# Six weight slots in place of four, with the low half of a weight unit written over its landed values

## The chip, the cores and the metric

One core of one Trainium2 chip runs the whole program. The metric is the device time of one execution, in microseconds (us). Matrix products run on TensorE (PE), copies and exponentials on ScalarE (ACT), elementwise work and reductions on VectorE (DVE) and GpSimd (POOL), and SyncE (SP) issues nearly all transfers from device memory. Every engine works through its own list of instructions in order and waits on semaphores where its program says so.

## The reference

Two layers, each with a combined input projection, three token mixers side by side, an output projection with a layer norm, and a squared-ReLU MLP with another. There are 512 tokens of width 1024, the input projection is 2578 wide, and the MLP 4096. Cut to what matters:

```python
for l in range(DEPTH):                                  # 2
    proj = jnp.einsum('btd,dn->btn', x, w_in[l])        # 1024 x 2578
    (qa, ka, va, u, qc, kcm, vcm, ksl, vsl, kwi, vwi, gc) = jnp.split(proj, offsets, axis=-1)
    qa = apply_rope(...); ka = apply_rope(...)
    o_a = diff_attention(qa[:, :, 0], qa[:, :, 1], ka[:, :, 0], ka[:, :, 1], va, lam, lam_init, subln_g[l])
    o_b = pool_mixer(u, w_pool[l], pool_scale[l])
    qc, kcm, ksl, kwi = (apply_rope(...) for each)
    o_c = nsa_attention(qc, kcm, vcm, ksl, vsl, kwi, vwi, gates, cmp_pe_k[l], cmp_pe_v[l], w_cmp_k[l], w_cmp_v[l])
    mix = jnp.einsum('btm,md->btd', jnp.concatenate([o_a, o_b, o_c], axis=-1), w_out[l])   # 1024 x 1024
    x = layer_norm(ALPHA * x + mix, ln1_g[l], ln1_b[l])
    hid = jnp.square(jax.nn.relu(jnp.einsum('btd,df->btf', x, w_up[l])))                   # 1024 x 4096
    x = layer_norm(ALPHA * x + jnp.einsum('btf,fd->btd', hid, w_down[l]), ln2_g[l], ln2_b[l])
```

`diff_attention` subtracts two causal softmaxes, weighted by `lam`, before it multiplies with the values. With 512 tokens, `N_SEL` covers every block and the window every key, so the selected and the window branch are plain causal attention.

## The kernel before

**Precision.** Every large product is made of three: a value is split into a high part (`w_hi`, `xt_hi`, rounded to the matmul's type) and a low part (value minus high part), and PE adds high x low, high x high and low x high.

**Weight units.** The weights of a layer are cut into 96 units (`UNITS`) of 256 rows by 430 columns (input projection, units 0 to 23) or by 512 (output projection 24 to 31, MLP 32 to 95). Four units make a chunk of output columns. A unit goes through three places: SP loads it into `raw` (L398 to L420), ACT writes `w_hi` from it (`split_to`, L880 to L888), and POOL writes `w_lo` as `raw` minus `w_hi` (`split`, L483 to L490). Each of the three has `RING` = 4 slots of 4 KB per partition, and unit g (counted through both layers) uses slot g modulo `RING`. Units 26, 27, 30 and 31 are loaded in three, two, three and two transfers, the others in one.

**What frees a slot.** Before the change, the load of unit g waits until POOL has written the low part of unit g-4 (`s_lo_ready`); ACT and POOL wait until PE has used unit g-4 (`s_unit_used`, one count for each unit that PE is through with). The program writes "PE is through with n units" as `unit_used` n; so here below too, counted within the layer.

**Order on ACT.** In the input projection (L936 to L945) step n first splits all units below n+`RING` and then, where n is a multiple of four or one more (from 4 on), copies two of the four PSUM banks of the chunk that PE has ended (`copy_in`). At n = 4, ahead of the splits of that step, it copies the turned parameters to `lnp` and `pe_t` (L939, L940); PE waits for that before its second chunk (L807). The last chunk's four banks follow (L946 to L951), then two copies to `ka` (L956), one exponential of `lams` (L959), the splits up to `U_OUT + RING` (L960), and then the attention tasks, of which `exps(t)` is the first part of each.

**Order on DVE.** DVE rotates the positions (`rotate`) of the A heads after the second chunk is copied, and those of the C heads after the fifth chunk is copied (L1180). Behind that come the copies of the turned queries and keys (L1189, L1191), two small operations on `lams` (L1194, L1195) and then `negative_max(0)` and `(1)` (L1201), for which the first `exps` wait. `weights(t)` (L1246 for the first member of a pair, L1244 for the second) scales the probabilities.

**Order on POOL.** It splits the units up to `U_OUT + RING` and then makes the rows for the compressed keys and values (`rows_to_compress`, L508), rotations, box sums and masks during attention. In the MLP loop ACT splits one unit and copies one block of the hidden layer (L1067) in turns.

Of the kernel before, what the change touches and what calls it, by code (L numbers as in the profile page):

```python
# [16 lines left out]
F32R = mybir.dt.float32r  # L17
# [40 lines left out]
IN_W, IN_CHUNKS = 430, 6  # L58
U_IN, U_OUT, U_MLP = 0, 24, 32
UNITS = U_MLP + 4 * N_MLP  # L60
RING = 4
TURN_BANK = (4, 0)

PARTS = ((0, 1), (2,), (3,))
# [84 lines left out]
def pieces(u):  # L149

    return {U_OUT + 2: 3, U_OUT + 3: 2, U_OUT + 6: 3, U_OUT + 7: 2}.get(u, 1)
# [20 lines left out]
def build(nc, x, w_in, lam_q1, lam_k1, lam_q2, lam_k2, subln_g, w_pool, pool_scale, cmp_pe_k, cmp_pe_v,  # L172
          w_cmp_k, w_cmp_v, w_out, ln1_g, ln1_b, w_up, w_down, ln2_g, ln2_b, consts, out):
    ctx = ExitStack()
    with ctx:
        top = [16512]

        def at(name, offset, shape, dt=F32):

            return nc.alloc_sbuf_tensor_at(name, [P] + list(shape), dt, offset=offset)  # L180

        def room(nbytes):
            top[0] += nbytes
            return top[0] - nbytes

        def sb(name, shape, dt=F32):
            size = int(np.prod(shape)) * (2 if dt == BF16 else 4)
            return at(name, room((size + 31) // 32 * 32), shape, dt)
# [5 lines left out]
        ident16 = sb("ident16", [P], BF16)  # L194
        mask16 = sb("mask16", [P], BF16)
        xres = sb("xres", [TT, D])
        raw = sb("raw", [RING, 1024])
        w_hi = sb("w_hi", [RING, 1024], F32R)
        w_lo = sb("w_lo", [RING, 1024], F32R)

        ra = room(32768)
        xt_hi, xt_lo = at("xt_hi", ra, [KT, SEQ], F32R), at("xt_lo", ra + 16384, [KT, SEQ], F32R)
# [64 lines left out]
        def sem(name):  # L267
            return ctx.enter_context(nc.semaphore(name))

        def raw_landed(layer, u):  # L270

            before = layer * sum(pieces(v) for v in range(u % RING, UNITS, RING))
            return 16 * (before + sum(pieces(v) for v in range(u % RING, u + 1, RING)))

# [3 lines left out]

        s_raw = [sem(f"raw{r}") for r in range(RING)]
        s_ident_in = sem("ident_in")  # L280
# [10 lines left out]
        s_lo_ready = sem("lo_ready")  # L291
        s_unit_used = sem("unit_used")
# [62 lines left out]
        def unit_of(ring, u):  # L355

            return ring[:, u % RING].rearrange("p (k c) -> p k c", k=2)[:, :, 0:unit_width(u)]

        def unit_source(layer, u):
            kind, c = CHUNKS[u // 4]  # L360
            r = 256 * (u % 4)
            if kind == "in":
                src = w_in[layer, r:r + 256, IN_W * c:IN_W * c + unit_width(u)]
            elif kind == "out":
                src = w_out[layer, r:r + 256, 512 * c:512 * c + 512]
            elif kind == "up":
                src = w_up[layer, r:r + 256, 512 * c:512 * c + 512]
            else:
                r += 1024 * (c // 2)
                src = w_down[layer, r:r + 256, 512 * (c % 2):512 * (c % 2) + 512]  # L370
            return src.rearrange("(k p) c -> p k c", p=P)
# [27 lines left out]
        def _(sp):  # L399
            sp.dma_start(ident, consts[:, K_ID:K_ID + P]).then_inc(s_ident_in, 16)  # L400
            def unit(layer, u):
                g = layer * UNITS + u
                if g >= RING:

                    sp.wait_ge(s_lo_ready, g - RING + 1)
                to = unit_of(raw, u)
                cols = slice(512 * CHUNKS[u // 4][1], 512 * CHUNKS[u // 4][1] + 512)
                if pieces(u) == 1:
                    sp.dma_start(to, unit_source(layer, u)).then_inc(s_raw[u % RING], 16)
                elif pieces(u) == 3:  # L410

                    sp.dma_start(to[:, 0], w_out[layer, 512:640, cols]).then_inc(s_raw[u % RING], 16)
                    for hh in range(2):
                        r = 640 + 192 * hh
                        sp.dma_start(to[64 * hh:64 * hh + 64, 1], w_out[layer, r:r + 64, cols]).then_inc(s_raw[u % RING], 16)
                else:
                    for hh in range(2):
                        r = 704 + 192 * hh
                        sp.dma_start(to[64 * hh:64 * hh + 64], w_out[layer, r:r + 128, cols].rearrange("(k p) c -> p k c", p=64)) \
                            .then_inc(s_raw[u % RING], 16)  # L420

            for layer in range(DEPTH):
                for u in range(RING):
                    unit(layer, u)
                    if layer == 0 and u == 0:
                        for tt in range(TT):
                            sp.dma_start(xres[:, tt], x[0, tt * P:(tt + 1) * P, :]).then_inc(s_x_in[tt], 16)
# [25 lines left out]
                for u in range(RING, UNITS):  # L453
                    if u == 3 * RING:
                        if layer:

                            sp.wait_ge(s_out_normed, nth("out_normed", layer - 1, TT))
                        else:

                            sp.wait_ge(s_masks, 1)  # L460
                        sp.dma_start(cmp_kw[:, :, 1, :], w_cmp_v[layer].rearrange("(j h) d e -> (h d) j e", h=2)) \
                            .then_inc(s_value_weights, 16)
                    unit(layer, u)
# [915 lines left out]
```

## Time and profile before

| | |
|---|---|
| time, median of 3 runs | 1374.91 us (1374.71 to 1378.96) |
| the profiled execution's own time | 1374.61 us |
| its span from the first to the last instruction | 1372.8 us |
| PE busy | 1290.0 us (94%) |
| DVE busy | 728.4 us (53%) |
| POOL busy | 568.6 us (41%) |
| ACT busy | 486.3 us (35%) |
| DMA moved | 110.03 MB, 80 GB/s on average |

The time and the span are 1.8 us apart. A share of busy time is an average over stages that have different limits: in the projections and the MLP PE works without a gap, in the attention (about 128 to 285 us and 804 to 965 us) and around the layer norms it waits for others. Times in the views count from the start of the span. "Granted clock" is the share of TensorE's full 2.4 GHz that the chip allowed in a stretch: 1.00 or, at the lower level of 1.2 GHz, 0.50.

### The profile page before, as it was taken

What the parts mean: (1) busy time and instruction counts of PE and PEld (TensorE: products, weight loads), DVE (VectorE), ACT (ScalarE), POOL (GpSimd) and SP (SyncE); (2) the same over time, 40 slices, a digit from 0 to 9 for tenths busy, and PEclk for the clock granted to TensorE, in tenths of its full rate; (3) what the DMA queues carried; (4) which work ended last, traced back from release to release, by engine and by line L of the source; (5) the groups of instructions that cost most, each with busy time, mean ns of one, the idle gap of its engine ahead of it and who ended that gap; (6) DMA issues with size and microseconds to landing.
All of it is one profiled execution on the core that took longest, in us unless ns stands there. A gap on an engine that the chain in (4) does not pass through costs nothing.

```text
span 1372.8 us, 17332 instructions
## 1 busy us (share of the span) xinstructions
PE 1290.0 (94%) x6834; PEld 1060.2 (77%) x6834; DVE 728.4 (53%) x1107; ACT 486.3 (35%) x1016; POOL 568.6 (41%) x320
## 2 busy tenths in 40 slices
PE   7999878998999999999989978899989999999996
PEld 6998545687888888888889965556888888888885
DVE  4234796717865063360495077866288641623506
ACT  4234557713322222221233345586233222222211
POOL 4443840033644444444355449100436444444444
PEclk9999689999999999999999987799999999999998
DMA  7432100021422322322144320000314232233211
GB/s 253 117 95 76 33 1 1 1 93 62 137 94 93 105 94 93 103 97 90 39 131 111 98 78 0 1 1 1 111 43 154 92 106 95 93 102 98 93 62 61
DMA packets 66656, 110.03 MB, mean 80 GB/s; under 512 B 14928, under 2 KB 27536, under 8 KB 66448
## 3 DMA queue, kind: packets, MB, share of 16 engines
q1 hardware_dynamic: 65424, 104.74, 24.5%
q10 hardware_dynamic: 1152, 4.19, 0.9%
q8 instruction: 54, 0.88, 0.3%
q14 instruction: 26, 0.21, 0.1%
HBM read 106.82 MB, written 2.10 MB: 79 GB/s over the span
## 4 chain that ended last, share of the span: by engine, by line
PE 86%; DVE 9%; ACT 2%; POOL 1%; issue 1%; DMA 1%; SPq 0%; POOLq 0%; ACTq 0%; DVEq 0%
PE ps L650 16%; PE ps L651 16%; PE ps L652 16%; PE ps L646 8%; PE ps L648 8%; PE ps L647 8%; PE ps L709 3%; PE ps L701 3%; DVE probs_a L1244 2%; PE ps L745 2%; DVE negmax L1201 1%; PE ps L605 1%; PE ps L730 1%; DVE xres L1111 1%; DVE probs_a L1246 1%; PE ps L761 1%
## 5 line engine op out<-in xcount | busy, mean ns | idle before, releaser
L489 POOL TENSOR_TENSOR w_lo<-raw,w_hi 128x1024 fp32r<-128x1024 f32 (+2 forms) x192 | 461.8, 2410 | 709.8 <-ACT w_hi L887 709.7
L887 ACT ACTIVATE w_hi<-raw 128x1024 fp32r<-128x1024 f32 (+2 forms) x192 | 196.4, 1026 | 619.8 <-PE ps L652 387.2
L646 PE MATMUL ps<-xt_hi,w_lo 128*128 128x512 f32 (+1 forms) x576 | 212.5, 369 | 8.8 <-DVE xt_lo L1092 8.8
L647 PE MATMUL ps<-xt_hi,w_hi 128*128 128x512 f32 (+1 forms) x576 | 211.7, 368 | 0.0
L648 PE MATMUL ps<-xt_lo,w_hi 128*128 128x512 f32 (+1 forms) x576 | 211.6, 367 | 0.0
L650 PE MATMUL ps<-w_hi,mt_lo 128*128 128x512 f32 x384 | 150.4, 392 | 0.0
L652 PE MATMUL ps<-w_lo,mt_hi 128*128 128x512 f32 x384 | 149.5, 389 | 0.0
L651 PE MATMUL ps<-w_hi,mt_hi 128*128 128x512 f32 x384 | 149.5, 389 | 0.0
L650 PE MATMUL ps<-w_hi,xt_lo 128*128 128x430 f32 (+1 forms) x384 | 138.9, 362 | 6.2 <-DVE xt_lo L1092 4.5
L651 PE MATMUL ps<-w_hi,xt_hi 128*128 128x430 f32 (+1 forms) x384 | 138.0, 359 | 0.0
L652 PE MATMUL ps<-w_lo,xt_hi 128*128 128x430 f32 (+1 forms) x384 | 137.8, 359 | 0.0
L646 PEld LDWEIGHTS ps<-xt_hi,w_lo 128*128 128x128 f32 x576 | 110.0, 191 | 27.0 <-DVE xt_lo L1092 8.1
L647 PEld LDWEIGHTS ps<-xt_hi,w_hi 128*128 128x128 f32 x576 | 110.0, 191 | 17.6
L648 PEld LDWEIGHTS ps<-xt_lo,w_hi 128*128 128x128 f32 x576 | 109.8, 191 | 17.4
L1302 DVE TENSOR_TENSOR xres<-xres,ps 128x512 f32<-128x512 f32 x48 | 32.9, 685 | 137.4 <-PE ps L652 136.6
L650 PE MATMUL ps<-w_hi,he_lo 128*128 128x512 f32 x256 | 99.6, 389 | 0.0
L651 PE MATMUL ps<-w_hi,he_hi 128*128 128x512 f32 x256 | 99.6, 389 | 0.0
L652 PE MATMUL ps<-w_lo,he_hi 128*128 128x512 f32 x256 | 99.6, 389 | 0.0
L1330 DVE TENSOR_TENSOR mt_lo<-tmp,mt_hi 128x512 fp32r<-128x512 f32 x32 | 71.3, 2229 | 47.9 <-ACT mt_hi L1067 47.9
L1201 DVE TENSOR_REDUCE negmax<-ps 128x2 f32<-128x256 f32 (+2 forms) x96 | 76.6, 819 | 37.1 <-PE ps L701 36.5
L1338 DVE TENSOR_SCALAR tmp<-ps 128x512 f32<-128x512 f32 x64 | 44.1, 689 | 89.6 <-PE ps L648 88.5
L1330 DVE TENSOR_TENSOR he_lo<-tmp,he_hi 128x512 fp32r<-128x512 f32 x32 | 65.6, 2049 | 40.2 <-ACT he_hi L1067 40.2
(164 smaller groups left out, 1977.1 us busy)
## 6 DMA issues: line engine op xcount, KB each, us to landing
raw<-in_w_up SPq DMA_DIRECT2D x64, 512.0 KB, 3.7
raw<-in_w_down SPq DMA_DIRECT2D x64, 512.0 KB, 3.7
raw<-in_w_in SPq DMA_DIRECT2D x40, 430.0 KB, 3.5
raw<-in_w_out SPq DMA_DIRECT2D x8, 512.0 KB, 3.7
raw<-in_w_in SPq DMA_DIRECT2D x8, 428.0 KB, 3.3
raw<-in_w_out SPq DMA_DIRECT2D x12, 256.0 KB, 3.8
xres<-in_x SPq DMA_DIRECT2D x4, 512.0 KB, 6.0
rows<-in_ln_g ACTq DMA_DIRECT2D x4, 512.0 KB, 4.2
```

The source lines that it names most:

```text
L489: nc.gpsimd.tensor_tensor(unit_of(w_lo, u), unit_of(raw, u), unit_of(w_hi, u).bitcast(F32), ALU.subtract).then_inc(s_lo_ready, 1)
L646: mm(o, wl[:, c], a_hi[:, k, cols], start=first, stop=False)
L647: mm(o, wh[:, c], a_hi[:, k, cols], start=False, stop=False)
L648: return mm(o, wh[:, c], a_lo[:, k, cols], start=False, stop=end)
L650: mm(o, a_lo[:, k, c], wh, start=first, stop=False)
L651: mm(o, a_hi[:, k, c], wh, start=False, stop=False)
L652: return mm(o, a_hi[:, k, c], wl, start=False, stop=end)
L701: last = mm(o[:, at_:at_ + n], queries, keys, start=False, stop=True, skip_group_check=True)
L887: A(unit_of(w_hi, u), unit_of(raw, u), ACT.Copy).then_inc(s_hi_ready, 1)
L1201: last = V.tensor_reduce(negmax[:, t % 2, a, :], ps[:, b:b + 2, at_:at_ + n], AX.X, ALU.max, negate=True)
L1330: V.tensor_tensor(lo[:, f], tmp[:, f % 2], hi[:, f].bitcast(F32), ALU.subtract) \
L1338: link(V.tensor_scalar(tmp[:, f % 2], ps[:, bank + b, :], 0.0, None, ALU.max))
```

## The change

`RING` becomes 6. `raw` and `w_lo` are two names for the same memory (`rw`), so that POOL's subtraction writes over the values that it reads. Six slots of two buffers take the same 48 KB per partition as four slots of three, so nothing else moves in memory. Since `w_lo` is what PE reads, the load of unit g must now wait until PE has used unit g-6.

```diff
-RING = 4
+RING = 6
...
-        raw = sb("raw", [RING, 1024])
         w_hi = sb("w_hi", [RING, 1024], F32R)
-        w_lo = sb("w_lo", [RING, 1024], F32R)
+        rw = room(RING * 4096)
+        raw, w_lo = at("raw", rw, [RING, 1024]), at("w_lo", rw, [RING, 1024], F32R)
...
                 if g >= RING:
 
-                    sp.wait_ge(s_lo_ready, g - RING + 1)
+                    sp.wait_ge(s_unit_used, g - RING + 1)
```

Every place that counts with `RING` moves: ACT's step n splits unit n+5 where it split unit n+3. Both wait for the same count of `unit_used`, but the load of unit n+5 itself now starts only at that count.

The first place is ACT in the first chunk, from the last block scaled by `lnp` (L898) to the first copy of the projection. Before:

```order
L887 ACTIVATE w_hi<-raw 128x2x430 [waits unit_used,raw0,const_in]
L887 ACTIVATE w_hi<-raw 128x2x430 [waits unit_used,raw1]
L887 ACTIVATE w_hi<-raw 128x2x430 [waits unit_used,raw2]
L939 ACTIVATE lnp<-ps 128x32 [waits par_turned]
L940 ACTIVATE pe_t<-ps 128x64
L887 ACTIVATE w_hi<-raw 128x2x430 [waits unit_used,raw3]
```

And after the change (`rawN` is the semaphore of a landed load into slot N):

```order
L887 ACTIVATE w_hi<-raw 128x2x430 [waits raw4,const_in]
L887 ACTIVATE w_hi<-raw 128x2x430 [waits raw5]
L887 ACTIVATE w_hi<-raw 128x2x430 [waits unit_used,raw0]
L887 ACTIVATE w_hi<-raw 128x2x430 [waits unit_used,raw1]
L887 ACTIVATE w_hi<-raw 128x2x430 [waits unit_used,raw2]
L939 ACTIVATE lnp<-ps 128x32 [waits par_turned]
L940 ACTIVATE pe_t<-ps 128x64
L887 ACTIVATE w_hi<-raw 128x2x430 [waits unit_used,raw3]
```

Two more splits stand ahead of L939 and L940: units 4 to 8 where units 4 to 6 stood.

The second place is ACT where it copies out the fifth chunk of the input projection, banks 0 and 1 first and then 2 and 3. Before:

```order
L927 ACTIVATE proj_b<-ps 128x8
L927 ACTIVATE proj_b<-ps 128x64
L927 ACTIVATE proj_b<-ps 128x128 x2
L927 ACTIVATE proj_b<-ps 128x102
L887 ACTIVATE w_hi<-raw 128x1024 [waits unit_used,raw0]
L927 ACTIVATE proj_b<-ps 128x8 [waits unit_used]
L927 ACTIVATE proj_b<-ps 128x64
L927 ACTIVATE proj_b<-ps 128x128 x2
L927 ACTIVATE proj_b<-ps 128x102
```

And after:

```order
L927 ACTIVATE proj_b<-ps 128x8
L927 ACTIVATE proj_b<-ps 128x64
L927 ACTIVATE proj_b<-ps 128x128 x2
L927 ACTIVATE proj_b<-ps 128x102
L887 ACTIVATE w_hi<-raw 128x1024 [waits unit_used,raw2]
L927 ACTIVATE proj_b<-ps 128x8 [waits unit_used]
L927 ACTIVATE proj_b<-ps 128x64
L927 ACTIVATE proj_b<-ps 128x128 x2
L927 ACTIVATE proj_b<-ps 128x102
```

The split between the two pairs is that of unit 24 (slot 0) before, and of unit 26 (slot 2 of six) after, which comes in three transfers.

## Rows read from the trace of the kernel before

**Rows 1.** Waits of PE: who was waited for, us in total, times, longest.

```profile
PE ps L709 <- DVE probs_a L1244: 31.3, 12, 5.9
...
PE ps L650 <- POOL w_lo L489: 0.9, 1, 0.9
```

**Rows 2.** Waits of SP's queue, same columns.

```profile
SPq L409 <- POOL w_lo L489: 1160.7, 173, 156.0
```

**Rows 3.** Transfers: issues of 24 to 40 us, median us to landing; then line L415.

```profile
raw<-in_w_in SPq DMA_DIRECT2D x4, 430.0 KB, 3.4
...
DMA to landing us min/median/max: 2.9/3.2/3.4
```

**Rows 4.** Timeline of ACT, first layer: start us, us, engine, line, operation, shapes, idle before.

```profile
30.79 0.93 ACT L887 ACTIVATE w_hi<-raw 128x860 fp32r<-128x860 f32 x1 [1.40 <-PE ps L652]
...
33.45 0.22 ACT L940 ACTIVATE pe_t<-ps 128x64 f32<-128x64 f32 x1
```

**Rows 5.** Timeline of PE, first layer, start of the second chunk.

```profile
33.72 0.46 PE L650 MATMUL ps<-w_hi,xt_lo 128*128 128x430 f32 x1 [0.40 <-ACT pe_t L940]
```

**Rows 6.** The same place in the second layer: timelines of ACT and PE.

```profile
707.02 0.93 ACT L887 ACTIVATE w_hi<-raw 128x860 fp32r<-128x860 f32 x1 [1.05 <-PE ps L652]
...
709.95 0.46 PE L650 MATMUL ps<-w_hi,xt_lo 128*128 128x430 f32 x1 [0.40 <-ACT pe_t L940]
```

**Rows 7.** Timeline of SP's queue: the three transfers of unit 26.

```profile
107.94 0.34 SPq L412 DMA_DIRECT2D raw<-in_w_out  x1
108.33 1.11 SPq L415 DMA_DIRECT2D raw<-in_w_out  x2
```

**Rows 8.** Timeline of ACT, last chunk of the input projection and start of attention.

```profile
114.24 1.06 ACT L887 ACTIVATE w_hi<-raw 128x1024 fp32r<-128x1024 f32 x1 [2.39 <-PE ps L652]
...
133.72 0.35 ACT L997 ACTIVATE probs_a<-ps,negmax 128x128 f32<-128x128 f32 x1
```

**Rows 9.** Timeline of DVE in the same stretch.

```profile
116.74 1.79 DVE L385 TENSOR_TENSOR tmp<-proj_b,kc 128x192 f32<-128x192 f32 x4 [35.97 <-ACT proj_b L927]
...
128.61 1.50 DVE L1189 COPY qkt<-ps 128x512 f32<-128x512 f32 x2 [1.20 <-PE ps L819]
...
131.34 0.15 DVE L1194 TENSOR_TENSOR lams<-lams 128x1 f32<-128x1 f32 x1
...
131.88 2.12 DVE L1201 TENSOR_REDUCE negmax<-ps 128x2 f32<-128x256 f32 x4 [0.21 <-PE ps L701]
135.46 0.18 DVE L1228 RECIPROCAL recs<-sums 128x4 f32<-128x4 f32 x1 [1.45 <-ACT probs_a L997]
135.67 3.94 DVE L1246 TENSOR_SCALAR probs_a<-probs_a,recs 128x128 f32<-128x128 f32 x4
```

**Rows 10.** Timeline of POOL, start of attention, narrow windows.

```profile
134.31 2.35 POOL L489 TENSOR_TENSOR w_lo<-raw,w_hi 128x1024 fp32r<-128x1024 f32 x1
...
136.61 2.35 POOL L489 TENSOR_TENSOR w_lo<-raw,w_hi 128x1024 fp32r<-128x1024 f32 x1
...
139.55 6.42 POOL L522 TENSOR_TENSOR cmp_wv<-qkt,pe_t 64x248 f32<-64x248 f32 x8
```

**Rows 11.** Timeline of DVE: operations beside POOL's, and one without.

```profile
136.66 2.38 DVE L1246 TENSOR_SCALAR probs_a<-probs_a,recs 128x128 f32<-128x128 f32 x1
...
717.88 2.03 DVE L1169 TENSOR_TENSOR bst<-lamv 128x32 f32<-128x32 f32 x1
...
720.16 0.19 DVE L1171 TENSOR_TENSOR bst<-lamv 128x32 f32<-128x32 f32 x1
```

**Rows 12.** Timeline of DVE while POOL is idle.

```profile
189.48 1.01 DVE L1246 TENSOR_SCALAR probs_a<-probs_a,recs 128x128 f32<-128x128 f32 x4
...
193.80 1.41 DVE L1244 SCALAR_TENSOR_TENSOR probs_a<-probs_a,facs 128x128 f32<-128x128 f32 x4
```

**Rows 13.** Timeline of PE: the first turn of probabilities.

```profile
144.63 1.54 PE L709 MATMUL ps<-kc,probs_a 128*128 128x128 f32 x6 [4.27 <-DVE probs_a L1244]
```

**Rows 14.** Waits of DVE in the MLP, columns as in rows 1.

```profile
DVE tmp L1338 <- PE ps L648: 88.5, 14, 18.9
```

**Rows 15.** Stretches: from:to us, length, PE busy (matmuls), granted clock, DMA share, GB/s.

```profile
134.00:136.00 2.00, 0.43 (x4) 0.50 0.28 37
...
156.00:158.00 2.00, 2.00 (x12) 0.53 0.00 0
```

## The prediction

> **What bounds the kernel now.** I read PE's waits first, since PE is busy for 94% of the span. They say that weights bound nothing: PE waited once for a low part, 0.9 us [rows 1], during the start. The largest wait is for DVE's `weights` in attention, 31.3 us [rows 1]. Then SP's queue: its loads sat 1160.7 us behind POOL's splits [rows 2], so before the change a load is issued long before its slot is wanted, and ACT finds it landed; what ACT waits for is PE's count. So two more slots have no weight wait to remove. What is left is what the later loads do to the work that stands behind them. For that I read the timelines of ACT, DVE and POOL at the second chunk of each layer and at the start of attention.
>
> **The new wait.** Step n of ACT waited for `unit_used` n. It still does, and now for the landing of a load that starts at that count too. A one-transfer load of the input projection lands 3.4 us after its issue (median), a piece of unit 26 after 2.9 to 3.4, median 3.2 [rows 3]. SP reacts in hundredths. ACT executes its list in order, so everything behind such a split comes 3 to 4 us later. PE itself needs the unit five units on, over 20 us away, so the weights are in time; I cost that at nothing, and if a landing took 15 us it would still be covered. That leaves three kinds of work behind the splits.
>
> **Part 1, `pe_t` ahead of the second chunk.** At n = 3 ACT splits unit 6 at 30.79 as soon as PE has counted three; the copies to `lnp` and `pe_t` then wait for PE, the last starts at 33.45 and takes 0.22, and PE resumes at 33.72 [rows 4, 5]. After the change the same place is the split of unit 8, whose load is issued at 30.79. It lands at 34.19; the next ACT operation can start some 0.83 later (I take 35.02), `pe_t` starts 0.1 after `lnp` and ends at 35.34, and PE resumes at 35.39. That is 1.67 us later than 33.72. The second layer has the same picture, from 707.02 to 709.95 [rows 6]: 707.02 + 3.4 + 0.83 + 0.32 + 0.05 = 711.62, again 1.67. Nothing hides it: PE has only this chunk to do. **Sum 3.3 us**. From below, a landing of 2.9 us, the fastest piece seen, gives 1.2 each. From above, 4 us gives 2.3 each, 4.6 in all.
>
> **Part 2, copies of the fifth chunk, then DVE's rotations.** At n = 21 ACT splits unit 24 at 114.24, with no wait for data, copies banks 2 and 3, and DVE starts on the C heads at 116.74 [rows 8, 9]. After the change unit 26 stands there. Its three issues take 0.39 (from 107.94 to 108.33) and then half of 1.11 before the third starts [rows 7], 0.95 together, and that lands 3.2 later: 118.4. So DVE starts 4.15 us later, at 120.9. The rotations ended at 127.41 (128.61 less the idle 1.20 [rows 9]); now at 131.56. The idle 1.20 hides that much. From the first copy to L1194 it took 131.34 - 128.61 = 2.73, so L1194 comes at 131.6 + 2.73 = 134.3 to 134.4.
>
> There it meets POOL. The three splits of POOL stand where they were (units 27 to 29 for 25 to 27; unit 29's load is issued when PE ends the chunk at about 128.0 and has landed before ACT reaches its split at 132.8), with boundaries at 134.31, 136.61 and 138.91 [rows 10]. DVE operations with two operands in SBUF wait for the end of POOL's operation: the 128x32 of L1169 took 2.03 beside POOL, its twin L1171 took 0.19 without it, and the second block of L1246 took 2.38, from 136.66 to the end of POOL's third split [rows 11]. L1194 and L1195 are of that kind, and L1195 waits for L1194. Before, they ran at 131.34, just ahead of POOL. If L1194 arrives after 134.31 it runs at 136.6 and L1195 at 138.9 (**late**); if before, at 134.31 and 136.6 (**early**). The arrival falls on the boundary within the spread of a landing; I take late, since semaphores to ACT and DVE add some hundredths that I have left out.
>
> Late: `negmax` starts at 139.1 and its first half takes 1.06, so the first `exps` starts at 140.2 in place of 133.72 [rows 8], 6.5 later. Some comes back. Before, the four blocks of L1246 took 3.94 beside POOL [rows 9]; now POOL has ended its splits and waits for a copy of ACT that comes later too, so they take 1.01 [rows 12]. DVE then waits for the next scores: `negmax(2)` starts at about 144.1 and L1244 at 145.35. Its four blocks, which would take 1.41 with POOL idle [rows 12], meet POOL's next work (it started at 139.55 [rows 10], now some 6.5 later) with the last one only, so they end near 147.3. PE's first turn of probabilities stood at 144.63 [rows 13] and now stands at 147.3: 2.7 us late. In the early case all of it is 2.3 to 2.4 less: 0.3 us late. The second layer has the same offsets. **Late 5.4 us for both layers, early 0.6.**
>
> POOL's list in attention is then some 2 us later relative to DVE's than it was, since it also gives up a pause. No one waits for its results (they come with over 5 us to spare), but as much of DVE's work at the end of the list runs beside POOL instead of after it. Beside POOL the paired operations took 1.4 to 3.9 times as long as alone [rows 9, 12]; an estimate of **0.7 us for each layer, 1.4 in all**, between 0 and 2 each.
>
> **Part 3, the rest.** In the MLP the copies of the hidden layer stand behind the splits and come 4 us later; DVE's low parts follow. DVE has slack there (it waited 88.5 us, up to 18.9 at a time, for PE at the next block [rows 14]), and a down chunk reads hidden blocks at least one chunk old. Nothing. In the layer norms the splits that collide with DVE stand where they stood, since their loads are issued 15 us or more earlier. At the start, units 4 and 5 now go ahead of constants and parameters, which then come some 3 us later and are needed at 33 us; nothing. The in-place subtraction reads and writes as much as before; nothing, and if it were slower by a tenth of a microsecond PE would not see it.
>
> **The sum.** 3.3 + 5.4 + 1.4 = 10.1 on the profiled execution's 1374.61, which is 0.3 below the median of the runs: **1384.7 us**. Early: 3.3 + 0.6 + 1.4 = 5.3, so 1379.9; one layer of each kind 1382.3.
>
> Of the landing, the Trainium skill ("SBUF — State Buffer", "The DMA setup-cost knee") says that a transfer takes about 2 us plus its bytes at 436 GB/s. For the last piece of unit 26 (128 KB) that would be 2.3 us where the trace has 3.2; by that figure L1194 would come 0.9 us sooner, at 133.4, the early case would hold in both layers, and the time would be an estimate of 1379 us. The trace's durations decide.
>
> **Rivals.** *Early in one or both layers* (1379.9 to 1382.3): for it, the margin is under 0.1 us; against it, the hundredths left out. *The clock falls in the new stall.* PE now stands still for some 2 us at the second chunk. The row at 134 us has the clock at 0.50 after PE had nothing but small products and a 2.6 us idle; at 156 to 158 it comes back [rows 15]. If the fall happens at both second chunks, PE runs at half speed for some 3 us there, 1.5 to 2 us more each: about 1388. Against it, PE works densely up to the stall. *The clock comes back sooner in attention*, the case on the other side: from 134 to 158 PE is at half clock [rows 15], with some 18 us of busy time in each layer. The new start shifts the busy stretch; each microsecond of that work at full clock saves half. It decides from 20 us of work at full clock for both layers together, where the 10.1 us are paid back; all 36 us would give 1384.7 - 18 = 1367. Against it, PE's idle before that stretch gets longer, not shorter. *The change does nothing*: the landing is hidden after all, because ACT is late at both places anyway; but ACT's rows show that it had waited 1.40 and 2.39 us for PE there [rows 4, 8]. It would give 1374.6.
>
> **How the numbers follow.** Late in both layers 0.40; early or mixed 0.32; clock in the stall 0.13 (1386 to 1390); no effect 0.05; clock back sooner 0.05 (1367 to 1380, half of it below 1370.5); something dearer, such as attention's collisions with POOL falling worse, 0.05. A measurement can tell about 0.3%, 4.1 us, from no change: slower is over 1379.0. Of the early cases a tenth falls below that. So slower 0.86, same 0.10, faster 0.04. The range from 1378.5 to 1389 holds the first three cases with their bounds (3.3 down to 2.4 and up to 4.6; the collisions 0 to 4).
>
> **What would show it.** Right: PE's wait for `pe_t` near 2.1 us in each layer; DVE's rotation of the C heads starting about 4 us later after PE's count; L1194 or L1195 with 2 us each; the first `exps` 4 to 6.5 us later; ACT's splits released by a DMA instead of PE. Wrong: a landing that delays nothing, a turn of probabilities at the old distance from the end of the projection, or a change of the granted clock between the projection and the middle of attention. PE waiting for `w_lo` or `w_hi` in the MLP would refute part 3.

## The result and the profile after

Over 17 runs of each, the changed kernel takes 1382.63 us (median, 1377.1 to 1384.87) and the kernel before 1377.05 us (1372.03 to 1382.46). The ratio is 1.0034, with a 95% interval from 1.0019 to 1.0050: 4.7 us slower, between 2.6 and 6.9. In a second measurement on other occasions the ratio was 1.0051 (1.0030 to 1.0072). The direction and the range held; the sum of 10.1 us was about double the first measurement. The change is small beside the spread between executions of one kernel (12.8 us between the fastest and the slowest of the changed one's second measurement), so only ratios over many runs can show it, and a single time can't.

The page of the profiled execution (1382.63 us): span, busy time and, for 40 slices, busy tenths of VectorE and the granted clock.

```profile
span 1380.8 us, 17329 instructions
...
PE 1298.4 (94%) x6834; PEld 1065.9 (77%) x6834; DVE 756.5 (55%) x1107; ACT 484.0 (35%) x1016; POOL 565.2 (41%) x320
...
PEclk9999779999999999999989987799999999999998
```

PE waits for weights as little as before; what is new is the third row below (the wait for `pe_t`), which stood at 0.8 us for both layers before. Waits of PE (us in total, times, longest):

```profile
PE ps L709 <- DVE probs_a L1244: 20.2, 12, 5.6
PE ps L691 <- ACT probs_a L997: 11.9, 4, 5.4
...
PE ps L650 <- ACT pe_t L940: 3.7, 2, 1.8
...
PE ps L650 <- POOL w_lo L489: 1.2, 1, 1.2
```

ACT now waits for transfers where it waited for PE. Waits of all engines:

```profile
ACT w_hi L887 <- DMA raw<-in_w_down: 261.0, 64, 4.8
ACT w_hi L887 <- DMA raw<-in_w_up: 199.4, 52, 7.0
...
ACT w_hi L887 <- DMA raw<-in_w_in: 119.3, 40, 7.1
```

**The second chunk, first layer.** The answer to [rows 4, 5], from the timelines of PE and ACT: the split of unit 8 waits for its landing, `pe_t` follows, and PE stands from its parameter turns (33.05) to 35.17.

```profile
33.05 0.28 PE L805 MATMUL ps<-kc,pe_raw 32*128 32x32 f32 x2
35.17 0.46 PE L650 MATMUL ps<-w_hi,xt_lo 128*128 128x430 f32 x1 [1.83 <-ACT pe_t L940]
...
33.99 0.92 ACT L887 ACTIVATE w_hi<-raw 128x860 fp32r<-128x860 f32 x1 [1.34 <-DMA raw<-in_w_in]
34.82 0.18 ACT L939 ACTIVATE lnp<-ps 128x32 f32<-128x32 f32 x1
34.90 0.22 ACT L940 ACTIVATE pe_t<-ps 128x64 f32<-128x64 f32 x1
```

**The second chunk, second layer.** The same (compare [rows 6]), and behind it the granted clock falls. From the timeline of PE and from the stretches (length, then for each engine its busy time and instructions, granted clock, DMA share, GB/s):

```profile
714.82 0.28 PE L805 MATMUL ps<-kc,pe_raw 32*128 32x32 f32 x2
716.93 0.49 PE L650 MATMUL ps<-w_hi,xt_lo 128*128 128x430 f32 x1 [1.83 <-ACT pe_t L940]
717.23 0.55 PE L651 MATMUL ps<-w_hi,xt_hi 128*128 128x430 f32 x1
717.59 0.56 PE L652 MATMUL ps<-w_lo,xt_hi 128*128 128x430 f32 x1
...
716.00:718.00 2.00, 1.07 (x4) 1.00 (x5) 2.00 (x1) 0.88 (x3) 2.00 (x2) 0.81 0.69 212
718.00:720.00 2.00, 2.00 (x7) 1.87 (x6) 2.00 (x2) 1.76 (x3) 2.00 (x1) 0.50 0.00 0
720.00:722.00 2.00, 2.00 (x10) 1.90 (x10) 1.97 (x2) 0.00 (x0) 2.00 (x2) 0.84 0.00 0
```

Products start 0.36 us apart at half clock where they started 0.19 apart: seven in two microseconds. By the clocks of the three rows (0.81, 0.50 and 0.84 over 2 us each) PE was at half clock for 3.4 us.

**The start of attention, first layer.** The answers to [rows 7 to 10], from SP's queue, ACT, DVE and POOL in turn:

```profile
114.41 0.34 SPq L412 DMA_DIRECT2D raw<-in_w_out  x1
114.79 1.11 SPq L415 DMA_DIRECT2D raw<-in_w_out  x2
...
118.33 1.06 ACT L887 ACTIVATE w_hi<-raw 128x1024 fp32r<-128x1024 f32 x1 [2.52 <-DMA raw<-in_w_out]
...
138.18 0.37 ACT L997 ACTIVATE probs_a<-ps,negmax 128x128 f32<-128x128 f32 x1 [3.95 <-DVE negmax L1201]
...
120.82 1.80 DVE L385 TENSOR_TENSOR tmp<-proj_b,kc 128x192 f32<-128x192 f32 x4 [35.75 <-ACT proj_b L927]
...
131.54 1.29 DVE L1189 COPY qkt<-ps 128x512 f32<-128x512 f32 x2
...
133.94 0.84 DVE L1194 TENSOR_TENSOR lams<-lams 128x1 f32<-128x1 f32 x1
134.82 2.27 DVE L1195 TENSOR_TENSOR lams<-lams,kc 128x1 f32<-128x1 f32 x1
137.12 1.95 DVE L1201 TENSOR_REDUCE negmax<-ps 128x2 f32<-128x256 f32 x4
...
140.14 1.01 DVE L1246 TENSOR_SCALAR probs_a<-probs_a,recs 128x128 f32<-128x128 f32 x4
...
132.41 6.95 POOL L489 TENSOR_TENSOR w_lo<-raw,w_hi 128x1024 fp32r<-128x1024 f32 x3 [10.55 <-ACT w_hi L887]
```

The split of unit 26 waits for its three transfers, DVE starts 4.1 us later, its copies end with POOL in the first of its splits, and L1194 and L1195 end with the first and the second of them: 3.1 us for two operations on one column. The first exponential comes at 138.18 in place of 133.72. Then the four blocks of L1246 take 1.01 in place of 3.94. The end of the projection (first turn L819) and the first turn of probabilities (L709) stand as follows, the first row in the kernel before, the others in the changed kernel:

```profile
127.91 2.78 PE L819 MATMUL ps<-kc,proj_a 128*128 128x128 f32 x24
...
128.32 2.78 PE L819 MATMUL ps<-kc,proj_a 128*128 128x128 f32 x24
...
145.24 1.54 PE L709 MATMUL ps<-kc,probs_a 128*128 128x128 f32 x6 [0.41 <-DVE probs_a L1244]
```

That is 16.92 us apart, where before had 144.63 - 127.91 = 16.72. Counted from the end of the projection the first exponential is 4.1 us later (9.86 us behind it in place of 5.81), and of that 0.2 are left at the first turn. In the second layer it is the other way round, 16.92 us in place of 17.14. The three profiles of the kernel before (next table) have 16.71 to 17.18, so neither difference is more than its own scatter.

**Where the 8.0 us between the two spans lie.** I cut both timelines of PE at the same operations: the parameter turns (L805), the start of the second chunk, the end of the projection (L819), the first and the last turn of probabilities (L709), and the turns of the rows around the norms (L605). Distances in us, here and for the kernels of the next section; "look" is how many units ahead the splits go at steps 1 to 3 and at the later steps.

| kernel | look | stall 1 | chunks 2 to 6, layer 1 | end to first turn | attention, layer 1 | stall 2 | chunks 2 to 6, layer 2 | end to first turn | attention, layer 2 |
|---|---|---|---|---|---|---|---|---|---|
| before | 4, 4 | 0.69 | 94.19 | 16.72 | 134.89 | 0.68 | 94.19 | 17.14 | 137.98 |
| before, second profile | 4, 4 | 0.69 | 94.18 | 16.71 | 135.81 | 0.68 | 93.16 | 17.18 | 140.45 |
| before, third profile | 4, 4 | 0.69 | 93.17 | 17.13 | 137.79 | 0.69 | 93.17 | 17.14 | 137.40 |
| after | 6, 6 | 2.12 | 93.15 | 16.92 | 137.88 | 2.11 | 94.73 | 16.92 | 137.28 |
| after, second profile | 6, 6 | 2.21 | 94.19 | 16.93 | 140.01 | 2.41 | 95.99 | 16.93 | 139.76 |
| splits 4 ahead everywhere | 4, 4 | 0.68 | 94.19 | 16.65 | 137.43 | 0.69 | 94.19 | 16.71 | 135.87 |
| only steps 1 to 3 | 4, 6 | 0.68 | 93.17 | 16.92 | 137.74 | 0.69 | 93.17 | 16.91 | 140.08 |
| same, timed again | 4, 6 | 0.68 | 94.19 | 16.92 | 138.31 | 0.69 | 94.19 | 16.92 | 138.08 |
| only later steps | 6, 4 | 2.18 | 93.16 | 17.14 | 137.80 | 2.36 | 94.75 | 17.14 | 137.49 |
| lams later | 6, 6 | 2.28 | 93.16 | 17.20 | 137.63 | 2.30 | 94.73 | 16.88 | 137.76 |
| shared memory, four slots | 4, 4 | 2.33 | 93.17 | 16.91 | 137.99 | 2.21 | 94.73 | 16.91 | 133.60 |
| longer stall | 7, 6 | 4.70 | 95.31 | 16.93 | 137.59 | 4.60 | 96.28 | 16.95 | 139.85 |

The stall column holds whatever else moves. The attention columns do not: three profiles of one program, taken on three occasions, differ by 2.9 and 3.1 us there. So the 3.0 us that the first comparison shows in the first layer's attention, and the 0.7 us that it wins back in the second, are not read as effects.

The table leaves out the norms, and the first comparison differs there too. From the first L605 of the first layer's norm to that of the next it took 359.46 us before and 360.72 after, from there to L805 of the second layer 30.09 and 30.77, and from the second layer's first L605 of that kind to the end of the span 373.35 and 374.75. These 3.3 us are no effect that can be shown either: the second profile of the changed kernel has 359.24 in the first of these stretches, and the kernel before had up to 31.77 and 374.78 in the other two. So the 8.0 us are 2.9 of stalls, 2.3 of attention, 3.3 of norms and -0.5 of chunks 2 to 6, where the fall of the clock (1.6) and a quicker pace of PE's products (-1.0 in each layer, see the last section) add up. More than half of them is scatter, and it is by chance that scatter and effects have one sign here.

### The profile page after: what moved, and what is told of

Same layout as the page of the kernel before. It is cut to its first block, busy times and chain, and to the rows that moved or that the text cites. A ratio compares the mean times of both kernels' runs of the same rounds, so it can differ in the third digit from the quotient of the medians.

```text
span 1380.8 us, 17329 instructions
## 1 busy us (share of the span) xinstructions
PE 1298.4 (94%) x6834; PEld 1065.9 (77%) x6834; DVE 756.5 (55%) x1107; ACT 484.0 (35%) x1016; POOL 565.2 (41%) x320
## 4 chain that ended last, share of the span: by engine, by line
PE 83%; DVE 11%; ACT 2%; DMA 1%; issue 1%; POOL 1%; SPq 0%; POOLq 0%; DVEq 0%; ACTq 0%
PE ps L650 15%; PE ps L652 15%; PE ps L651 15%; PE ps L646 8%; PE ps L647 8%; PE ps L648 8%; PE ps L709 3%; PE ps L701 3%; DVE probs_a L1244 2%; DVE negmax L1201 2%; PE ps L745 2%; DMA raw<-in_w_in 1%; PE ps L605 1%; DVE xres L1111 1%; DVE tmp L385 1%
## 5 line engine op out<-in xcount | busy, mean ns | idle before, releaser
L1330 DVE TENSOR_TENSOR mt_lo<-tmp,mt_hi 128x512 fp32r<-128x512 f32 x32 | 79.0, 2469 | 54.2 <-ACT mt_hi L1067 54.2
L1330 DVE TENSOR_TENSOR he_lo<-tmp,he_hi 128x512 fp32r<-128x512 f32 x32 | 70.1, 2190 | 45.9 <-ACT he_hi L1067 45.9
```

Source lines behind the costliest of these rows:

```text
L1330: V.tensor_tensor(lo[:, f], tmp[:, f % 2], hi[:, f].bitcast(F32), ALU.subtract) \
```

## The experiments

**1. The same kernel before, two more profiles.** No edit.

> The kernel before, once more, for a second profile. It shows how far the same program's stretches differ from one execution to the next. If the granted clock falls and returns at fixed points of the program, the spans of attention agree within 0.3 us with the first profile; if not, they differ by 1 to 4 us, and single differences of that size between before and after mean nothing.

> The kernel before, a third profile, to see how far attention's length scatters with no change in the program: 134.9 and 135.8 us in the first layer so far, 138.5 and 140.5 in the second. If 137 to 140 us turn up in the first layer too, the 3 us that the changed kernel's profiles have there are no effect of the change.

They took 1378.89 and 1377.77 us in their one run each. The first layer's attention measured 134.89, 135.81 and 137.79 us, the second's 137.98, 140.45 and 137.40. What moves is where the granted clock falls and returns. One stretch (134 to 204 us: length, PE busy, clock, DMA share, GB/s) of before, its third profile, after, and after's second profile:

```profile
134.00:204.00 70.00, 52.10 (x344) 0.77 0.09 23
...
134.00:204.00 70.00, 56.17 (x344) 0.73 0.08 23
...
134.00:204.00 70.00, 55.95 (x346) 0.74 0.00 1
...
134.00:204.00 70.00, 58.93 (x340) 0.68 0.00 1
```

The second row is an unchanged program with nearly the clock of the changed one. Differences under 3 us in attention are therefore left out of every account here. 137.79 lies in the 137 to 140 that the expectation named, in which both profiles of the changed kernel fall.

**2. The changed kernel, a second profile.** No edit.

> The changed kernel again, unchanged, for a second profile. In the first profile PE's second chunk starts at 35.17 us where before had 33.72, the first turn of probabilities stands 0.2 us later than the end of the projection explains, and then 3.6 us more are lost between 158 and 204 us in the first layer but almost none in the second. If that later loss belongs to the order of the work (POOL's list running later beside DVE), it is there again in the first layer within 0.5 us. If it comes from where the granted clock falls and returns, it moves: another size in this profile, with the half-clock stretches at other places. The stalls at the second chunks (1.5 us each) and the late copies are the same in either case. Time: 1377 to 1385 us, 3 to 7 us over the kernel before.

1380.78 us (1375.24 to 1388.08), ratio 1.0051 (1.0030 to 1.0072). The stalls were there again (2.21 and 2.41), and so were the late copies, with 16.93 us to the first turn. The loss inside attention was not of the same size (137.88 and then 140.01), and it was there in the second layer as well. It moves with the clock.

**3. Splits four units ahead everywhere.** Memory and slots as changed:

```diff
-                    split_to(layer, n + RING)
+                    split_to(layer, n + RING - 2)
...
-                split_to(layer, U_OUT + RING)
+                split_to(layer, U_OUT + RING - 2)
...
-                        split_to(layer, U_MLP + 4 * k + b + RING)
+                        split_to(layer, U_MLP + 4 * k + b + RING - 2)
```

and POOL's `U_OUT + RING` twice in the same way.

> Six slots and shared memory stay, but ACT and POOL split as far ahead as before (four units instead of six), in the projection, around attention and in the MLP, so each load is issued two units before the split that needs it. By my theory (the loss is made by splits that wait for a landing with other work behind them on ACT) PE's second chunk starts at 33.7 again, ACT's split of unit 24 is at about 114.2, DVE's C rotation at 116.7, and the time is that of the kernel before within 1.5 us. By the rival that the shared memory itself costs (the in-place subtraction, or loads that are issued later), some of the 4 to 6 us stays: 1379 us or more.

1375.31 us against 1374.88, ratio 0.9999 (0.9976 to 1.0022). PE and ACT at the second chunk:

```profile
33.12 0.28 PE L805 MATMUL ps<-kc,pe_raw 32*128 32x32 f32 x2
33.80 0.46 PE L650 MATMUL ps<-w_hi,xt_lo 128*128 128x430 f32 x1 [0.40 <-ACT pe_t L940]
...
33.44 0.20 ACT L939 ACTIVATE lnp<-ps 128x32 f32<-128x32 f32 x1 [2.92 <-PE ps L805]
```

The loss is gone with the six slots and the shared memory in place. So the in-place subtraction and the later issue of loads cost nothing that can be measured (the interval allows 3 us either way); how far ahead ACT splits does. DVE's C rotation started at 113.5, not at the 116.7 of the expectation. With six slots and a look of four, ACT's split of unit 24 needs the slot of unit 18, which PE had already left; it ran at 110.87, between the two pairs of copies, without a wait for PE's count. Nothing came of that head start: 16.65 and 16.71 us to the first turn.

**4. Undoing one half each.** The look of four for steps 1 to 3 alone, and for the later steps with the edge of attention alone:

```diff
-                    split_to(layer, n + RING)
+                    split_to(layer, n + (RING - 2 if n < 4 else RING))
```

```diff
-                    split_to(layer, n + RING)
+                    split_to(layer, n + (RING if n < 4 else RING - 2))
```

and, in the second, ACT's and POOL's splits at the edge of attention with `RING - 2` as in experiment 3.

> Only steps 1 to 3 of ACT in the input projection look four units ahead; everything else is the changed kernel. My theory: PE's second chunk starts at 33.7 and its wait for the parameters is 0.4 us again, but DVE's C rotation still starts about 4 us later than before (some 120.8) and L1194 and L1195 still take 3 us together. The rival, that late parameter transfers on SP's queue hold PE up there (units 4 and 5 go ahead of them), leaves the second chunk at 35.2.

> Steps 4 to 21 of ACT and the splits at the edge of attention look four units ahead, steps 1 to 3 and the MLP six. My theory: the second chunk still starts near 35.2, but DVE's C rotation starts within 0.5 us of before relative to PE's count (2.5 us after unit 21), L1194 and L1195 take 0.15 us each, and the first exponential stands at 134 us or so. The MLP's copies stay behind late splits; if they cost anything it shows here as a loss between 345 and 675 us that the kernel before does not have (rival: 2 to 4 us there).

Each had one run, of 1379.03 and 1381.55 us. Undoing steps 1 to 3 alone brings the stalls back to 0.68 and 0.69. The parameter transfers on SP's queue stand where the change put them, so that rival is out. The late copies stay: DVE's C rotation starts at 118.99, 7.6 us ahead of the end of the projection at 126.55 (before: 11.2 ahead), and L1194 and L1195 took 0.91 and 2.26. And the first turn still stands 16.92 us after the end. Undoing the later steps alone brings L1194 and L1195 back to 0.15 and 0.16 and the first exponential to 134.39 (DVE's C rotation at 113.81, early as in experiment 3 and not where it was expected), and the first turn then stands 17.14 us after the end of the projection, not sooner:

```profile
128.58 2.78 PE L819 MATMUL ps<-kc,proj_a 128*128 128x128 f32 x24
145.72 1.54 PE L709 MATMUL ps<-kc,probs_a 128*128 128x128 f32 x6 [5.68 <-DVE probs_a L1244]
```

So the late copies, the largest term of the forecast, cost nothing that can be told from the scatter: -0.2 to 0.2 us for each layer. The MLP, where this kernel splits six ahead, measured 342.73 us from the last L605 of one norm to the first of the next, against 342.74 before.

The first of the two was timed again:

> The kernel of the run with steps 1 to 3 looking four units ahead, now timed. If the stall at the second chunk and the clock that falls behind it in the second layer are the whole loss of the change (1.45 + 1.5 + 1.6 us by the stretches), the time is that of the kernel before within its interval, 0.998 to 1.002. If the late copies and the later splits around attention cost as much as I had forecast (5 to 7 us with the late branch, 2 with the early one), it stays 2 to 7 us above.

1378.41 us against 1375.3, ratio 1.0015 (0.9995 to 1.0035). That includes no change, and it lies below the changed kernel's 1.0034 and 1.0051, but the intervals overlap. By the expectation 2.1 us is the top of "the stalls are all" and the foot of "the late copies cost too", so time alone doesn't decide; a remaining cost of up to 5 us is not excluded by it. That the late copies cost nothing rests on the distances in the table.

**5. The small operations moved.** L1194 and L1195, with their wait, go from ahead of `negative_max(0)` to behind `weights(0)`.

> The changed kernel with the two small operations on lams (L1194, L1195) moved behind the first block of weights, where their result is first needed one task later. My theory: DVE's C rotation still starts at about 120.8 us, the copies end at 134.0, but the first maximum then starts at 134 instead of 137.1 us and the first exponential at 135 to 135.5 instead of 138.2. The blocks of L1246 then fall beside POOL's third split again and take 2 to 3 us instead of 1.0, so the first turn of probabilities moves by 1 us at most. If the delay of the first exponential were the cost, the turn would come 3 us earlier (rival).

One run, 1381.58 us. The first exponential came at 135.34 in place of 138.18. DVE (the same operations, with line numbers four lower in this kernel):

```profile
134.29 1.94 DVE L1197 TENSOR_REDUCE negmax<-ps 128x2 f32<-128x256 f32 x4
...
137.30 3.19 DVE L1242 TENSOR_SCALAR probs_a<-probs_a,recs 128x128 f32<-128x128 f32 x4
```

and the first turn stood 17.20 us after the end of the projection (16.92 with the operations in their place), in the second layer 16.88. Three microseconds of a visible wait were taken off the path and nothing came of it, because the scaling then ran beside POOL's third split.

**6. The sharing alone, with four slots.** `RING = 4` in the changed kernel.

> Four slots, but with raw and w_lo in the same memory and loads that wait for PE: the sharing alone, without the two extra slots. A split waits for a landing as in the changed kernel, with the same distance between the count and the load, so the stalls at the second chunks (PE at 35.2) and the late copies are all there. Units now have 3 units or 14 to 16 us from load to use for 3.4 + 0.9 + 2.1 us of work, so PE still waits for no weights in the projections. My theory: 3 to 8 us over before, about as the six slots. Rival: the two extra slots are what hides most of it, and this kernel is 15 us or more over before with waits of PE for w_lo.

1385.67 us (1378.28 to 1390.06) against 1378.16, ratio 1.0054 (1.0029 to 1.0078). The stalls are 2.33 and 2.21, and PE waits for no weights beyond the start. With experiment 3 this says that the stall comes from sharing (a load that can't start before PE's count) together with splits that go as far ahead as there are slots, not from the number of slots; the two extra slots hide nothing of it. The stalls and the clock make 4.7 us here, inside the interval of 4.0 to 10.8. The profiled execution was the fastest of seven, with the shortest second attention of the table, so the profile can't show where the rest of 7.4 us would lie.

**7. A longer stall.** Unit 9, whose load can start only when PE has ended the chunk, goes ahead of the parameter copies:

```diff
-                    split_to(layer, n + RING)
+                    split_to(layer, n + (RING + 1 if n < 4 else RING))
```

> The changed kernel with the suspected wait made longer: steps 1 to 3 of ACT look seven units ahead, so that unit 9, whose load starts only when PE has ended the first chunk, stands ahead of the parameter copies. My theory: from the turned parameters to PE's second chunk it takes 2.3 us more than in the changed kernel, some 4.5 us in both layers, and the granted clock falls behind it in the second layer as it did with 2.1 us, and now perhaps in the first too (1.6 us each time it does). Rival (the fall of the clock in the second layer has nothing to do with the stall): the same stretch up to the first turn stays at 93.2 to 94.2 us in the second layer.

One run, 1392.0 us. The first layer's stretches and PE's start there:

```profile
37.50 0.73 PE L650 MATMUL ps<-w_hi,xt_lo 128*128 128x430 f32 x1 [4.42 <-ACT pe_t L940]
...
36.00:38.00 2.00, 0.50 (x1) 0.50 (x2) 0.00 (x0) 1.67 (x5) 1.67 (x2) 0.50 0.00 0
38.00:40.00 2.00, 2.00 (x7) 1.84 (x7) 0.00 (x0) 0.29 (x1) 1.35 (x1) 0.50 0.00 0
```

The stalls are 4.70 and 4.60, as expected, and now the clock falls in both layers: chunks 2 to 6 take 95.31 and 96.28 us, 2.1 us more in each than at full clock and the same pace (93.16 and 94.19). That is over the 1.6 us expected; the clock stood at 0.50 already when PE resumed. The clock's fall in the second layer belongs to the stall: it is there in all six profiles with a stall of 2.1 us or more and in none of the six that the table has without. In the first layer it fell only behind the longer one: in none of five profiles with 2.1 to 2.3 us, and in the one with 4.7.

**8. A version that beats both.** The late copies' small cost pointed at what does hold the start of attention: three splits of ACT ahead of the first exponential and three of POOL beside L1246. PE needs those units only at the end of attention. In the kernel before:

```diff
-                split(layer, 2 if layer else 0, U_OUT + RING)
+                split(layer, 2 if layer else 0, U_OUT + 1)
...
-                split(layer, U_OUT + RING, U_MLP + 2)
+                split(layer, U_OUT + 1, U_MLP + 2)
...
-                split_to(layer, U_OUT + RING)
...
+                split_to(layer, U_OUT + RING)
                 copy_p(TASKS - 1)
```

> The kernel before, with its four slots, and the same three splits moved behind the last exponential of attention; nothing else. My theory: the same gain at the start of attention, 3 to 10 us in all under before, since L1194 and L1195 run ahead of POOL's work there anyway; the extra slots of e8_late add nothing (difference between the two under 2 us).

The same on the six slots, with experiments 3 and 5:

> A version meant to beat both: six slots, ACT and POOL four units ahead, L1194 and L1195 behind the first weights, and the three splits of units 25 to 27, which stand between the projection and the first exponential, moved behind the last exponential of attention (ACT and POOL), where PE needs them from about 280 us on. My theory: the first exponential no longer waits for three splits of 0.97 us on ACT, and L1246 takes 1.0 us instead of 3.9, so the turn of probabilities comes 2.8 + 2.9 = 5.7 us sooner at most after the end of the projection, in each layer; less what PE's own scores or the later scaling take over. Between 3 and 10 us under before. Rival, seen in the other runs: the distance from the end of the projection to the first turn stays near 16.7 to 17.2 whatever stands before it, because a late start of DVE is paid back by free blocks of L1246; then nothing is gained. A wait of PE for w_lo at the end of attention would take some back.

With four slots 1370.77 us, ratio 0.9921 (0.9892 to 0.9950); with six 1369.58, ratio 0.9943 (0.9921 to 0.9964), both against the kernel before at 1378.8. Both are faster than the kernel before, and so than the changed one, whose ratios to it are above 1; the intervals do not tell them apart. Four slots, ACT, DVE and then PE:

```profile
133.09 0.37 ACT L996 ACTIVATE probs_a<-ps,negmax 128x128 f32<-128x128 f32 x1 [1.96 <-DVE negmax L1201]
...
135.06 1.01 DVE L1246 TENSOR_SCALAR probs_a<-probs_a,recs 128x128 f32<-128x128 f32 x4
...
128.06 2.78 PE L819 MATMUL ps<-kc,proj_a 128*128 128x128 f32 x24
140.16 1.54 PE L709 MATMUL ps<-kc,probs_a 128*128 128x128 f32 x6 [0.41 <-DVE probs_a L1244]
```

From the end of the projection to the first turn it is 12.10 and 11.76 us in the two layers, 11.89 and 12.99 with six slots, against 16.7 to 17.2 in every kernel of the table: 4.6 and 5.4 us less than before's first profile. Most of it is POOL's: the scaling beside POOL was 2.9 us longer, while ACT's first exponential comes only 0.8 us sooner after the end of the projection, since it now waits for `negmax`. The splits at the end of attention (POOL from 275.77) made PE wait for nothing. Whether the rest of attention gives some of the gain back stays open: it measured 139.86 and 138.17 us with four slots and 138.49 and 144.86 with six, the last 4.4 us longer than any in the table, in an execution that was among the slowest of its eleven.

## Why the prediction was right, and where it was off

The time fell in the range and moved the way that was forecast, by half of what was forecast. Part 1 was right; part 2, the largest term, was wrong, and its own sign of being wrong came true: the turn of probabilities stood at the old distance from the end of the projection.

**Weights bound nothing: right.** No kernel that was run waits for a weight beyond the start, and two more slots gained nothing.

**Part 1, the stall: right in mechanism and size.** Forecast 1.67 us for each layer, measured 2.12 - 0.69 = 1.43 and 1.43, in the second profile 1.52 and 1.73. The landing was 0.2 us shorter than forecast (the split of unit 8 ran at 33.99 where 34.19 had been forecast). Experiments 4 and 7 shorten and lengthen the stall with one number.

**The clock in the stall: the rival, given 0.13, holds in one layer.** Chunks 2 to 6 of the second layer take 94.73 us beside 93.16 and, in the second profile, 95.99 beside 94.19, each compared at its own pace of PE's products: 1.6 to 1.8 us. It had been priced at 1.5 to 2 for each layer, and 3.4 us at half clock fits that. Why a stall of 2.1 to 2.4 us is enough in the second layer in five of five profiles, and one of 2.1 to 2.3 in the first in none of five, stays open. One difference is on record: in the changed kernel's first profile PE had been at full clock from the start of the span to the first stall (1.00 from 0 to 33 us), while in the second layer it came from half clock in the norm (0.52 from 693 to 700 us) to 1.00 from 702 to 714.

**Part 2, the late copies: every step was there, and the branch and the term were wrong.** DVE's rotation was forecast for 120.9 and came at 120.82. The branch was early in every profile with late copies (L1194 took 0.5 to 1.2 us, so it came that much ahead of the end of POOL's first split). Two things put it there. I took 2.73 us from the first copy to L1194, in which one copy of before had waited for PE; without that wait it takes 2.40. And PE's end of the projection, to which POOL's splits are tied, moved by 0.41, which the forecast of POOL's boundaries left out. So L1194 came 0.8 us ahead of the boundary, not 0.1 behind it. The size follows: 5.4 us forecast for late, 0.6 for early, +0.2 and -0.2 in the two layers measured (and in experiment 4 undoing it gained nothing). The early branch with its forecast of 1379.9, 5.3 us over the profiled execution, is close to the ratio's 4.7, but by luck: it holds 1.4 us that can't be seen and lacks the 1.6 of the clock.

The estimate from the Trainium skill ("SBUF — State Buffer", "The DMA setup-cost knee") had the early branch right, but its 2.3 us for the last piece of unit 26 took the page's rate for a transfer over all 16 ports, while this piece writes 64 of the 128 partitions. The pieces landed 2.9 to 3.1 us after their issue in the changed kernel (2.9 to 3.4 before), and the branch was decided by the two things above.

**The end of POOL's list, 1.4 us: not shown.** It is smaller than attention's scatter of 3 us between profiles of one program. The 3.0 us that the first layer showed looked like it, and experiments 1 and 2 took that reading away.

**Part 3: right.** The MLP took the same 342.7 us. The kernel with splits four ahead answers for the in-place subtraction.

**The sum.** Stalls 2.9, the clock behind the second 1.6, the late copies nothing: 4.5 us, where the ratio says 4.7 (2.6 to 6.9). The forecast reached its 10.1 by one right term, one that was mis-sized by 5 us in the branch on which I had put 0.40, and one that can't be seen. The clock, left out of the sum, gave 1.6 instead. That the median of 1382.63 lies only 2.1 us under the forecast 1384.7 is partly luck: the forecast stood on 1374.61, and the kernel before measured 1377.05 in the same comparison.

## What to carry to other kernels

When a load buffer is shared with something that the matrix engine reads, the number of slots is no measure of how early data come: any instruction that now waits for a landing delays all that stands behind it on its engine, so look there first, and split fewer units ahead than there are slots. A delay in front of an engine that next collides with another may cost nothing, and a visible wait that is removed may gain nothing: ask when the collision ends, and move the colliding work itself. Before a difference of a few microseconds is explained, profile the unchanged kernel again: here that took away most of the 8.0 us between the first two profiles.

## What the runs showed of the hardware

- PE's dense products had two paces at a granted clock of 1.00 throughout. Chunks 2 to 6 of the same program took 94.19 us in one profile and 93.17 in another, with 410 and 415 matmuls on record in the same 80 us. Both paces turned up in kernels before and after the change; what sets them stays open. From before and its third profile:

```profile
40.00:120.00 80.00, 80.00 (x410) 1.00 0.37 101
...
40.00:120.00 80.00, 80.00 (x415) 1.00 0.37 104
```

- An operation of VectorE on a single column, with both operands in SBUF, took 2.27 us beside GpSimd's subtraction and 0.16 without it; the reciprocal beside the same work took 0.18. The Trainium skill ("SBUF — State Buffer", "SBUF: two separate sides") says that such an operation blocks for the whole of GpSimd's instruction when that started first and reads SBUF; the trace agrees: L1194 and L1195, one behind the other, took 0.84 and 2.27 us, each ending within 0.02 us of the end of a GpSimd split.
